# Gate and up products turned so that tokens are the output's partitions, with seven block products for two of eight tile pairs, and 12 seven-product units instead of 17 in the down product

## The reference

```python
h = h + rmsnorm(merged @ w_out[i], post_mix_g[i])
u = rmsnorm(h, pre_ffn_g[i])                                    # 256 tokens x 2048 are needed
ff = (jax.nn.silu(u @ w_gate[i]) * (u @ w_up[i])) @ w_down[i]   # 2048 x 5632, twice, then 5632 x 2048
h = h + rmsnorm(ff, post_ffn_g[i])
return h[:, N_META:]
```

## Time and profile before

| | |
|---|---|
| time, three runs | 1100.93 us median (1100.17 to 1101.36) |
| the profiled execution | 1101.34 us, of which the profiled span is 1099.4 us |
| PE busy | 1087.4 us, 99% of the span |
| VectorE, ScalarE busy | 792.1 us (72%), 558.7 us (51%) |
| weights loaded, gate, up, down | 88 chunks each, 512 KB, 4.4 to 4.5 us to landing |
| gate and up on PE | from 369.3 us to about 862 us |

### The profile page before, as it was taken

How to read it: one execution, slowest core, us unless ns; L and a number is a source line. 1 busy time by engine, 2 the same in 40 slices (tenths; PEclk the granted TensorE clock), 3 DMA queues, 4 the chain that set the end, 5 groups by cost and what they waited for, 6 DMA issues and landing times. The chain is left out here.

```text
span 1099.4 us, 17529 instructions
## 1 busy us (share of the span) xinstructions
PE 1087.4 (99%) x6461; PEld 966.1 (88%) x6461; DVE 792.1 (72%) x991; ACT 558.7 (51%) x695; POOL 27.3 (2%) x46
## 2 busy tenths in 40 slices
PE   9999999999999999999999999999999999999997
PEld 8999999999888888888888888888888888888885
DVE  5699896637646776666567766666566789978987
ACT  6554554736644664444444444444444555556553
POOL 4001001001000000000000000000000000000000
PEclk9999999999999999999999999999999999999999
DMA  7655444534486386656665666566666665656664
GB/s 266 212 172 173 154 123 148 155 113 154 126 314 192 117 282 195 190 176 195 188 188 170 205 194 188 176 194 190 189 190 188 233 208 176 225 180 218 210 206 184
DMA packets 155422, 207.72 MB, mean 189 GB/s; under 512 B 6368, under 2 KB 133792, under 8 KB 154096
## 3 DMA queue, kind: packets, MB, share of 16 engines
q1 hardware_dynamic: 153904, 199.38, 57.2%
q10 hardware_dynamic: 896, 6.30, 1.4%
q0 software_dynamic: 576, 1.40, 0.4%
HBM read 202.86 MB, written 4.19 MB: 188 GB/s over the span
## 5 line engine op out<-in xcount | busy, mean ns | idle before, releaser
L888 DVE TENSOR_TENSOR w_lo<-raw,w_hi 128x1024 fp32r<-128x1024 f32 x351 | 428.0, 1228 | 226.2 <-ACT w_hi L513 225.5
L513 ACT ACTIVATE w_hi<-raw 128x1024 fp32r<-128x1024 f32 x351 | 370.1, 1059 | 390.0 <-PE ps L1406 244.2
L1404 PE MATMUL ps<-u,w_hi 128*128 128x512 f32 x1408 | 491.2, 392 | 0.8 <-DVE u L996 0.8
L1406 PE MATMUL ps<-u,w_lo 128*128 128x256 f32 x1408 | 394.9, 281 | 0.0
L1404 PEld LDWEIGHTS ps<-u,w_hi 128*128 128x128 f32 x1408 | 264.1, 188 | 60.4 <-issue 1.1
L1406 PEld LDWEIGHTS ps<-u,w_lo 128*128 128x128 f32 x1408 | 265.3, 188 | 0.0
L1389 PE MATMUL ps<-u,w_hi 128*128 128x272 f32 (+1 forms) x544 | 158.8, 292 | 0.0
L1391 PE MATMUL ps<-u,w_hi 128*128 128x272 f32 (+1 forms) x544 | 155.9, 287 | 0.0
L1392 PE MATMUL ps<-u,w_lo 128*128 128x272 f32 (+1 forms) x544 | 155.7, 286 | 0.0
L1389 PEld LDWEIGHTS ps<-u,w_hi 128*128 128x128 f32 x544 | 102.4, 188 | 0.4
L1391 PEld LDWEIGHTS ps<-u,w_hi 128*128 128x128 f32 x544 | 102.5, 188 | 0.2
(11 more groups left out here) (256 smaller groups left out, 1052.5 us busy)
## 6 DMA issues: line engine op xcount, KB each, us to landing
raw<-in_w_gate SPq DMA_DIRECT2D x88, 512.0 KB, 4.5
raw<-in_w_up SPq DMA_DIRECT2D x88, 512.0 KB, 4.4
raw<-in_w_down SPq DMA_DIRECT2D x88, 512.0 KB, 4.5
raw<-in_w_in SPq DMA_DIRECT2D x72, 512.0 KB, 3.9
raw<-in_w_out SPq DMA_DIRECT2D x32, 512.0 KB, 4.7
arena<-in_x SPq DMA_DIRECT2D x2, 1024.0 KB, 6.1
arena<-in_x ACTq DMA_DIRECT2D x2, 1024.0 KB, 8.1
out<-h2rows ACTq DMA_DIRECT2D x2, 1024.0 KB, 7.6
```

What stands on the lines that cost most here:

```text
L513: act.activation(w_hi[:, slot, :], raw[:, slot, :], ACT.Copy).then_inc(hi_done, 1)
L888: dve.tensor_tensor(w_lo[:, slot, :], raw[:, slot, :], hi_view(w_hi[:, slot, :]), ALU.subtract).then_inc(lo_done, 1)
L1404: pe.matmul(ps[:, bank + m, :].rearrange("p (a t) -> p a t", a=2), w_hi[:, slot, at], u[:, kt, :, 0:SEQ], start=first and k == 0, stop=Fal ...
L1406: mm = pe.matmul(ps[:, bank + m, 0:SEQ], w_lo[:, slot, at], u[:, kt, 0, 0:SEQ], start=False, stop=last and k == len(kts) - 1, skip_group_c ...
```

## The change

Gate and up now take the form of the down product. The 5632 columns of gate and up are cut into 11 groups of 512 (`NFG`), each of 16 chunks, a chunk being one K tile by 512 columns of gate and 512 of up (two loads of 256 KB). A 128 x 128 tile of `u` is stationary and the weights move, 512 columns an instruction. The groups and the two down passes are numbered g = 0 to 12 and share one table `ROUND`: group 0 has no Z, groups 1 to 10 have two Z of eight pairs (20 units), the down passes have 5 and 7 (12 units, before 8 and 9). The result has tokens on partitions: ACT takes silu of each gate quarter with the norm as its per-partition scale (`silu`), DVE multiplies with up (`inner_product`), and PE turns this product by 8 transposes a group (`turn_inner`), 11 times, placed before the fourth chunk of the next group. The loops over the blocks are written out. The orders in the transition are new, its unused products are gone, and its first turn stands before the last chunk of the output projection.

```diff
-    Y0, Y1 = 8, 13
-    SEVEN_Y, SEVEN_U = tuple(range(Y0, Y1)), (13, 14, 15, 16)
-    SUM_AT = {9: 13, 15: 14, 20: 15, 24: 16}
...
+    SEVEN_F, SEVEN_U = (0, 1), (13, 14, 15, 16, 17, 18, 19)
+    SUM_AT = {4: 13, 11: 14, 13: 15, 19: 16, 21: 17, 27: 18, 29: 19}
...
-    ROUND = ("PPPZPPZPPZPZPZPZPZPZPP", "PPPZPZPZPZPZPZPZPZPZPP")
...
+    F_SUM_AT = {12: 0, 14: 1}
+    ROUND = ["PPPPPPPP"] + ["PPPZPZPP"] * (NFG - 1) + ["PPPPZPPPZPPPZPPPZPPZPP", "PPPZPPZPPZPPZPPZPZPZPP"]
...
-        def quarter(n, m, j):
-
-            return ps[:, 4 * ((n + 1) % 2) + 2 * m + j, :]
...
+        def quarter(g, m, j):
+
+            return ps[:, 4 * (g % 2) + 2 * j + m, :]
+
+        def sevens_bank(g, k):
+
+            return ps[:, 4 * ((g + 1) % 2) + k, :]
...
+            for q in range(Q_FFN, END):
+                g, ch, d = place_of(q)
+                kt = 2 * d + ch % 2
+                sp_eng.wait_ge(lo_done, q - WSLOTS + 1)
+                if g < NFG:
+                    for j, src in enumerate((wg_v, wu_v)):
+                        sp_eng.dma_start(raw[:, q % WSLOTS, j * DCOLS:(j + 1) * DCOLS],
+                                         src[:, kt, g * DCOLS:(g + 1) * DCOLS]).then_inc(raw_landed[q % WSLOTS], 16)
...
+            def silu(b):
+                for m in range(NQ):
+                    if b:
+                        act.wait_ge(fold_done, len(QUARTERS) * (b - 1) + m + 1)
+                    else:
+                        act.wait_ge(chunks_used, BEGIN[1])
+                        act.wait_ge(r2c_done, 1)
+                        act.wait_ge(h2_kept, 16 * NQ)
+                    act.wait_ge(p_done, NQ * b)
+                    act.activation(gated[:, m, :], quarter(b, m, 0), ACT.Silu, scale=r2c[:, m:m + 1]).then_inc(silu_done, 1)
+
+            def inner_hi(b):
+                act.wait_ge(f_turned, b + 1)
+                act.copy(ffn[:, 4 * b:4 * b + 4, 0, :],
+                         ps[:, 4 * (b % 2):4 * (b % 2) + 2, :].rearrange("p b (c t) -> p (b c) t", c=2)).then_inc(f_hi, 1)
...
+            def inner_product(b):
+
+                if b:
+                    for j in range(2):
+                        for m in range(NQ):
+                            fold(b, m, j)
+                for m in range(NQ):
+                    dve.wait_ge(silu_done, NQ * b + m + 1)
+                    dve.wait_ge(r2c_done, 1)
+                    if b:
+                        dve.wait_ge(fold_done, len(QUARTERS) * (b - 1) + NQ + m + 1)
+                        dve.wait_ge(f_turned, b)
+                    dve.scalar_tensor_tensor(inner[:, m, :], quarter(b, m, 1), r2c[:, m:m + 1], gated[:, m, :],
+                                             ALU.mult, ALU.mult).then_inc(p_done, 1)
+
+            def inner_lo(b):
+                dve.wait_ge(f_hi, b + 1)
+                dve.tensor_tensor(ffn[:, 4 * b:4 * b + 4, 1, :],
+                                  ps[:, 4 * (b % 2):4 * (b % 2) + 2, :].rearrange("p b (c t) -> p (b c) t", c=2),
+                                  hi_view(ffn[:, 4 * b:4 * b + 4, 0, :]), ALU.subtract).then_inc(f_lo, 1)
...
+            def fold(g, m, j):
+                dve.wait_ge(x_step, 4 * g)
+                if g < NFG:
+                    dve.wait_ge(chunks_used, BEGIN[g + 1])
+                dve.tensor_tensor(quarter(g, m, j), quarter(g, m, j), folded(g, m, j), ALU.add).then_inc(fold_done, 1)
...
-            turn(0, [0])
-            for _ in range(WARM_FFN):
-                pe.matmul(ps[:, 2, 0:SEQ], ffn[:, 0, 0, 0:P], ffn[:, 0, 0, :], start=True, stop=True)
-            pe.wait_ge(rows_done, 5)
-            turn(0, [1])
-
...
+            for s in range(OC):
+                if s == OC - 1:
+                    pe.wait_ge(rows_done, 1)
+                    turn(0, [0])
+                out_products(OUT_G - 1, s, [1]).then_inc(chunks_used, 1)
...
+            def plain_products(q, quarters):
+                g, ch, d = place_of(q)
+                kt, chs = 2 * d + ch % 2, 2 * len(ROUND[g])
                 pe.wait_ge(lo_done, q + 1)
-                pe.wait_ge(f_lo, kt // 2 + 1)
+                if g >= NFG:
+                    pe.wait_ge(f_lo, kt // 4 + 1)
                 for m, j in quarters:
-                    o = quarter(n, m, j)
...
+                    mm = three(quarter(g, m, j), left(g, kt, m), right(q, j), ch == 0, ch == chs - 1)
...
+                three(m1, left(g, 2 * d, 0), right(q, 0), begin, end).then_inc(chunks_used, 1)
                 pe.wait_ge(lo_done, q + 2)
-                three(quarter(n, 0, 0), row(0, 1), weight(1, 0))
-                three(quarter(n, 0, 1), row_sum(2), weight(1, 1)).then_inc(chunks_used, 1)
+                three(quarter(g, 0, 0), left(g, 2 * d + 1, 0), right(q + 1, 0))
+                three(quarter(g, 0, 1), row_sum(2), right(q + 1, 1)).then_inc(chunks_used, 1)
                 pe.wait_ge(t_lo_done, 2 * z + 1)
                 three(m5, row_sum(0), weight_sum(0), begin, end).then_inc(t_used, 1)
-                three(m7, row(1, 0), weight_sum(1), begin, end).then_inc(t_used, 1)
+                three(m7, row_sum(3) if g < NFG else left(g, 2 * d, 1), weight_sum(1), begin, end).then_inc(t_used, 1)
                 pe.wait_ge(t_lo_done, 2 * z + 2)
                 three(m6, row_sum(1), weight_sum(2), begin, end).then_inc(t_used, 1)
-                three(quarter(n, 1, 0), row(1, 1), weight_sum(3)).then_inc(t_used, 1)
-
-            for n in range(DW):
-                if n == 0:
-                    pe.wait_ge(down_free, 4)
+                three(quarter(g, 1, 0), left(g, 2 * d + 1, 1), weight_sum(3)).then_inc(t_used, 1)
...
+            def turn_inner(b):
+
+                pe.wait_ge(p_done, NQ * (b + 1))
+                for m in range(NQ):
+                    for t in range(4):
+                        at = t % 2 * SEQ + m * P
+                        mm = pe.transpose(ps[:, 4 * (b % 2) + t // 2, at:at + P], inner[:, m, t * P:(t + 1) * P], ident)
+                mm.then_inc(f_turned, 1)
+
+            pe.wait_ge(y_done, NQ * DN_OUT - 1)
+            for ch in range(2):
+                plain_products(Q_FFN + ch, [(0, 0), (0, 1)])
+            pe.wait_ge(rows_done, 3)
+            turn(0, [1])
+            pe.wait_ge(y_done, NQ * DN_OUT)
+            for ch in range(2):
+                plain_products(Q_FFN + ch, [(1, 0), (1, 1)]).then_inc(chunks_used, 1)
+            for ch in range(2, KT):
+                if ch in (2, 5, 7):
+                    quad = 1 + (2, 5, 7).index(ch)
+                    pe.wait_ge(rows_done, 2 + 2 * quad)
+                    turn(quad, [0, 1])
+                plain_products(Q_FFN + ch, QUARTERS).then_inc(chunks_used, 1)
+
+            for g in range(1, NG):
+                if g == 1:
+                    pe.wait_ge(h2_lo, CK + KT)
                 else:
-                    pe.wait_ge(x_step, 4 * n)
-                whole = DCH if n < DW - 1 else DCH - LAST
-                for e in range(whole):
-                    if (n, TURNS[n][e // 2]) not in SEVEN_NO:
-                        down_products(n, e, QUARTERS).then_inc(chunks_used, 1)
-                    elif e % 2 == 0:
-                        seven_products(n, e)
-            late = [(0, 0, DCH - LAST, DCH - 1), (0, 1, DCH - LAST, DCH - 1), (0, 0, DCH - 1, DCH), (0, 1, DCH - 1, DCH),
-                    (1, 0, DCH - LAST, DCH), (1, 1, DCH - LAST, DCH)]
-            for m, j, e0, e1 in late:
-                for e in range(e0, e1):
-                    if (m, j) == QUARTERS[-1] and e == DCH - 2:
+                    pe.wait_ge(x_step, 4 * (g - 1))
+                chs = 2 * len(ROUND[g])
+                for ch in range(chs if g < NG - 1 else chs - LAST):
+                    q = BEGIN[g] + ch
+                    if g <= NFG and ch == 3:
+                        turn_inner(g - 1)
+                    if (g, TURNS[g][ch // 2]) not in SEVEN_NO:
+                        plain_products(q, QUARTERS).then_inc(chunks_used, 1)
+                    elif ch % 2 == 0:
+                        seven_products(q)
```

More of the change, by code:

```diff
@@ new lines, in build_trunk @@
+    TURNS = [in_turn(g) for g in range(NG)]
+    SEVENS = [(g, d) for g in range(NG) for d, c in zip(TURNS[g], ROUND[g]) if c == "Z"]
+    SEVEN_NO = {gd: z for z, gd in enumerate(SEVENS)}
+    SEVENS_TO = [sum(1 for k, _ in SEVENS if k <= g) for g in range(NG)]
+    FOLD = [2 * ROUND[g].rindex("Z") + 1 if "Z" in ROUND[g] else -1 for g in range(NG)]
+    QUARTERS = [(0, 0), (0, 1), (1, 0), (1, 1)]
+    FOLDS_F = len(QUARTERS) * (NFG - 1)
+    assert DW == 2 and ROUND[NG - 1].endswith("P" * (LAST // 2)) and all(d in SUM_NO for d in SEVEN_U)
@@ L220, in build_trunk @@
         rd, c = carve(cst, c, NQ)
-        r2, c = carve(cst, c, SEQ)
         ra, c = carve(cst, c, NQ)
@@ L870, in _ @@
-                if q - 4 >= Q_DOWN and e == DCH - 1 and n == 0:
+                        if z is not None:
+                            weight_sums_hi(z)
+                    if 1 <= g <= NFG and ch == 3:
+                        silu(g - 1)
```

(47 more changed lines are left out.)

588 lines of the change are left out of this document (231 added, 357 removed).

## The result

The change made the kernel slower: 1107.80 us median (1107.02 to 1108.04, 4 runs) against 1100.56 of the kernel before beside it (4 runs), a ratio of 1.0064 with a 95% interval of 1.0046 to 1.0081. The forecast was 1093.7 us, its range 1090.5 to 1098.5. The chance given to slower was 0.08.

What follows compares the result with a forecast made beforehand. PE, busy 99% of the span, was taken as the bound through the number and spacing of its instruction starts. -10.7 - 13.6 + 3.4 + 8.7 + 4.5 + 0.5 = -7.2 us gave 1093.7 us, range 1090.5 to 1098.5.

Steps and rivals of the forecast that it cites:

- the form of gate and up: Gate and up: 2112 instructions at down's 226.8 ns replace 1408 pairs at 347.8 ns, gain 10.7 us.
- the Z: Gate and up: seven products, 20 units in ten groups each saving 3 instructions, gain 13.6 us.
- An instruction costs by its columns: Rival, gate and up: 231.9 ns an instruction, no gain from the form, 1104 us; chance 0.06.
- The Trainium skill's rule: Instruction spacing of columns / 2.4 + 2.5 ns: the form gains 1.8 us, time 1103; said to contradict the trace.
- The clock's fall: Rival, transition: PE's clock falls to its lower level, some 3 us of products take twice as long, 1097; chance 0.13.
- The transition's waits: Output projection to gate and up: five PE gaps, waits of 8.8 us; the transition in all loses 4.5 us.
- The units: Seven products in gate, up and down: each unit saves 3 instructions of 226.8 ns.
- DVE keeps up: Groups of gate and up: DVE needs 36.0 of PE's 43.0 us, 84%; waits put at 0.
- The turns: Turns of the product: 11 times 8 transposes at 0.79 us of PE, loss 8.7 us, no idle time ahead.
- Down: Down goes from 17 to 12 units: 15 instructions more, loss 3.4 us.
- the stores: Stores of h2rows near chunk 13, beside its load: loss 0.5 us, between 0 and 2.

Runs made afterwards that it cites:

- e1: The changed kernel with the FFN input kept in tiles of 256 columns (1024 bytes a half) instead of 272 (1088 bytes): 1096.51 us, ratio to before 0.9960.
- e4: The kernel of e1 with all tiles of the FFN input beginning 64 bytes later: 1108.12 us, one run.
- e5: The kernel of e1 with all tiles of the FFN input beginning 128 bytes later: 1107.3 us, one run.
- e12: The fastest kernel (1087.0 us) with the region of `ffn`, stationary in down and the output projection, beginning 64 bytes later: 1096.1 us, one run.
- e3: The changed kernel with splits 6 and 8 to 11 ahead of the high or low halves and squares they stood behind: 1102.64 us, ratio to before 1.0019.
- e9: The kernel of e1 with one unit (Z) instead of two in each group of gate and up: 1102.69 us, ratio to before 1.0016.
- e7: The changed kernel with the edits of e1 and e3 together: 1091.80 us, ratio to before 0.9913.

## Why the prediction was wrong

**The step that failed** is the first term, the form of gate and up: "After, a chunk has 12 instructions of 512 columns, the same columns in all: 2112 x 226.8". The row of down was taken for gate and up because the instructions have the same form. They differ in where the stationary tiles begin, and that is worth 5.9 ns a product: e1 gives it back, e4 and e5 take it away again by an offset alone, e12 brings it into down. What about the place counts is open, as said there. Together with the Z it was worth -12.1 us instead of -24.3. A spacing above 230 and a clock below 1.00 near 370 us had both been named as what would make the prediction wrong, and both came.

**The rival with nearly the right time was wrong in its reason.** "An instruction costs by its columns" had 231.9 ns and 1104. The measured spacing was near that, but with the tiles moved (e1) it was 226.7 in the same stage. That the two numbers lie close says nothing for its reason. The Trainium skill's rule ("TensorE: Matmul & The Clock Gate", section Back-to-back issue gap), 215.8 ns, fits neither 226.7 nor 233.3, and has no term for the place.

**The clock's fall**, a rival of 0.13 priced at 3 us, came about together with the spacing: twice, 3.1 us. The argument against it, that the clock held through 3.7 us of idle at the end, was drawn from one place; the two falls followed 2.9 us of work in 6, and 2.64 us of idle. The price of 3 us was meant for one fall, which cost 1.6; it came out by luck, since there were two. I had treated as exclusive two mechanisms that add, and so neither range nor chances held their sum.

**The transition's waits** were right in place and cause and 1.4 us too long together; e3 took two of them away by the order that the prediction had blamed. **The units** cost what was said: 6.8 us for ten (e9). **DVE keeps up**: PE doesn't wait in any of groups 1 to 10. **The turns** wait for nothing and cost 0.88 us instead of 0.79, since the product behind one takes 0.31 to the next start; 1.0 us in all. **Down** was right within 0.1 us, **the stores** within 0.5.

With the tiles moved, the rest of the prediction stands: e1 at 1096.5 is 2.8 us above the forecast, and the clock, the turns, the waits and the stores (3.1 + 1.0 - 1.4 - 0.5) are 2.2 of it.

## What to carry to other kernels

A row gives the cost of an instruction only for operands placed as in that row: when an edit makes another tensor the stationary operand, compare the bytes at which its tiles begin with those of the tensor whose spacing you use, and give them the same remainder by 256 if you can. Take the whole address for this, the start of the region included, and read the spacing again in the new trace: a multiple of 256 was slow here (e5). When an edit leaves TensorE with little work for some microseconds, price the lower clock as well as the wait, and add mechanisms that can occur together instead of ranking them. Splits or loads that the next chunk needs go ahead of long operations that nobody waits for yet.

## What the runs showed of the hardware

- The start-to-start time of back-to-back products (tile of 128 x 128 stationary, 512 columns moving, fp32r) depends on where the stationary tiles begin in their partition. It was 226.6 to 227.0 ns where they began 128 bytes behind a multiple of 256, as the moving weights did, and 232.4 to 233.4 ns where all began 64 or 128 bytes further on. Seen for two tensors and three stages. With a step of 1088 bytes the mean was 232.7 ns, though a fourth of the halves had the fast place.
- A pair with the weights stationary took 347.8 ns with the moving tile in two runs of 256 columns 1088 bytes apart, and 353.0 ns in the profiled execution of a program with one run of 512 columns; that program's times fell into two groups 8 us apart. What decides is open.
- The clock fell to its lower level near 372 us after 2.9 us of work in 6 us, and near 399 us after 2.64 us of idle; each fall cost 1.6 us. 14 unused products of 0.13 us each ahead of the first place kept it at 1.00 at both in the one execution with them. The five executions of e7, one program, differ in their mean clock (0.994 to 0.998).
